# One more merged pair in each half of w_out, with all of w_out's weight sums made earlier and read back from DRAM

## The chip, the cores and the metric

The kernel runs on one core of a Trainium2 chip. The metric is the device time of one execution in microseconds (us), here the median of three runs. The engines named below are PE (TensorE, matmuls; PEld is its loading of the stationary operand), DVE (VectorE), ACT (ScalarE), POOL (GpSimd) and SP, which only issues DMAs. SP works through its DMA issues and its waits in one order; a wait holds up everything that stands behind it.

## The reference

One decoder layer on 256 tokens of width 2048: two attentions side by side, gated and merged, a projection w_out, and a gated MLP.

```python
h = rms_norm(x, attn_norm_g)
proj = h @ w_in
(q_sb, k_sb, v_sb, q_ds, k_ds, v_ds, q_ix, k_ix, w_ix, g_sb, g_ds) = jnp.split(proj, IN_OFFSETS, axis=-1)
...
merged = (jax.nn.sigmoid(g_sb) * (o_sb @ w_branch[:SB_W])
          + jax.nn.sigmoid(g_ds) * (o_ds @ w_branch[SB_W:]))
x = x + merged @ w_out
h = rms_norm(x, ffn_norm_g)
u = causal_depthwise_conv(h @ w_up, conv_w, conv_b)
gate, val = jnp.split(u, 2, axis=-1)
x = x + (jax.nn.silu(gate) * val) @ w_down
```

## The kernel before

**Stages.** In order of time: a short start; five row blocks of w_in (two computed chunk by chunk, three with merged pairs); four column groups of w_in for the first attention's q and k ("heads"); eight column groups for the gates, with one head of each attention worked in between ("gates"); four groups of w_branch; w_out in two halves of 1024 columns; eleven groups of w_up; w_down.

**Products.** Every weight is split into a rounded part hi (by ACT) and a rest lo (by DVE), and every product of a 128 x 128 tile with 512 columns is three matmuls: hi with hi, the left side's rest with hi, hi with the weights' lo. The weights go through a pipeline of *chunks*, numbered through the whole kernel: SP loads a chunk of 512 KB into a raw buffer, ACT writes hi[c % 4], DVE writes lo[c % 4], PE uses both. ACT may write hi of chunk c only when PE has done chunk c - 4 (semaphore w_used), and DVE counts up lo_done. ACT and DVE run three chunks ahead of PE (AHEAD = 3). In the chunked stages SP may refill a raw buffer once lo of the chunk four before is done.

**Plain and merged pairs.** In three row blocks, w_out and w_down, the 16 (w_out) row tiles of the weights are taken in pairs. A *plain* pair is 2 chunks and 8 products (2 row tiles x 2 token halves x 2 column halves). A *merged* pair (kind "summed") does the same 2 x 2 x 2 block product with 7 products in 4 chunks: 1, 2, 2 and 2 products. It needs sums of the weights' four blocks (s13, s24: 4 x 128 x 512) and sums of the left side (left_m for w_out), and its partial results go to four "far" PSUM banks which are copied out and joined by DVE afterwards (far_copy, then out_sums, renamed out_far by the change).

**w_out before.** OUT_SUMMED = 3 merged and 5 plain pairs per half, in the order of OUT_ORDER. Each step's two row tiles are loaded whole (load_step) into six raw buffers: raw0 to raw3 and raw45m. DVE makes the weight sums between its lo's, in weight_sums, from the two raw tiles: one operation of 1024 columns and two of 512. x is loaded again into y by POOL, in quarters, each behind a count of w_used.

**Sums made ahead.** For w_down the sums are made long before they are used. In the gates and the first branch group SP loads the three pieces of a w_down pair into pre_gates (load_terms: 512 + 256 + 256 KB), DVE adds in place (weight_terms: three operations at j = 5, 6, 7 of gates_body), and SP stores 1 MB to the DRAM tensor sums. One such round goes with each group of eight chunks: load at j = 0, store at j = 6 of the next group's loads (gates_turn). The stages of w_up do the same with two buffers. In w_down a merged pair with stored sums loads 256 KB and three times 512 KB.

Of the kernel before, what the change touches and what calls it, by code (L numbers as in the profile page):

```python
# [29 lines left out]
def hybrid_layer(nc, x, positions, attn_norm_g, w_in, q_norm_g, k_norm_g, w_branch, w_out,  # L30
# [51 lines left out]
    OUT_SUMMED = 3  # L82
# [5 lines left out]
    def block_steps(orders, chunk, raw):  # L88

        table = []  # L90
        for b, order in orders.items():
            for kind, pair in order:
                made = pair if kind == "summed" else None
                table.append(Step(b, pair, made, chunk, raw + 2 * len(table)))
                chunk += 2 if made is None else 4
            assert chunk == BLOCK_END[b]
# [7 lines left out]
    OUT_ORDER = [[("plain", 4)] + turns(0, 5, 1, 6, 2, 3) + [("plain", 7)],  # L104
                 turns(0, 4, 1, 5, 2, 6) + [("plain", 3), ("plain", 7)]]
    ROW_STEPS = block_steps({b: ROW_ORDER for b in S_BLOCKS}, ROWS_AT[2], 0)
    ROW_RAWS = 2 * len(ROW_STEPS)
    OUT_STEPS = block_steps({b: OUT_ORDER[b - NB] for b in OUT_BLOCKS}, C_OUT, ROW_RAWS)
    OUT_RAWS = 2 * len(OUT_STEPS)
    PART = {s.chunk + k: (s, k) for s in ROW_STEPS + OUT_STEPS  # L110
            for k in range(2 if s.made is None else 4)}
    ROW_S = [s for s in ROW_STEPS + OUT_STEPS if s.made is not None]
    OUT_FIRST = OUT_STEPS[1]
    FAR_LAST = {b: [s for s in ROW_S if s.m == b][-1].chunk for b in BLOCK_END}
    ROW_LOADS = ROW_RAWS // (SLOTS + 2)
    ROW_SAVED = (C_HEADS - ROWS_AT[2]) // SLOTS - ROW_LOADS
    OUT_EXTRA = (OUT_RAWS - 2 * SLOTS) // (SLOTS + 2)
    OUT_SAVED = (C_UP - C_OUT) // SLOTS - OUT_EXTRA - 2
    ROW_SLOT = [(q + SLOTS) % (SLOTS + 2) for q in range(ROW_RAWS)]
    ROW_SLOT += [q if q < SLOTS else q % SLOTS if q >= OUT_RAWS - SLOTS else q % (SLOTS + 2)  # L120
                 for q in range(OUT_RAWS)]

    def first_turn(q):

        if q < ROW_RAWS:
            return ROWS_AT[2] // SLOTS if ROW_SLOT[q] < SLOTS else 0
        return C_OUT // SLOTS - ROW_SAVED if ROW_SLOT[q] < SLOTS else ROW_LOADS
# [33 lines left out]
    IN_GATES = len(GATE_SUMS)  # L161
    LAST_GROUP = STORED + 1
# [21 lines left out]
    def raw_turn(q):  # L184

        slot = RAW_SLOT[q]
        if slot < SLOTS:
            turn = C_DOWN // SLOTS - ROW_SAVED - OUT_SAVED
        else:
            turn = ROW_LOADS + OUT_EXTRA if slot < SLOTS + 2 else 0  # L190
        return turn + RAW_SLOT[:q + 1].count(slot)
# [32 lines left out]
    with ctx:  # L224
# [9 lines left out]
        def sem(name):  # L234
# [82 lines left out]
        ssum13 = [at("hsum13", [2 * GRP], 74 * KB), at("msum13", [2 * GRP], 64 * KB)]  # L317
        ssum24 = [at("hsum24", [2 * GRP], 78 * KB), at("msum24", [2 * GRP], 68 * KB)]
        raw45m = at("raw45m", [2, 2 * GRP], 72 * KB)
        raw_s = [raw + [at("raw4h", [2 * GRP], 82 * KB), at("raw5h", [2 * GRP], 199 * KB)],  # L320
                 raw + [raw45m[:, 0, :], raw45m[:, 1, :]]]
# [41 lines left out]
        pre_gates = at("pre_gates", [4 * GRP], 48 * KB)  # L363
        sums = nc.dram_tensor("sums", (len(SUM_ROWS) * P, 4 * GRP), f32, kind="Internal").ap()
        leftb = [at(f"leftb{b}", [1, 4, 2, P] if b == SINGLE else [2, 3, 2, P], left_at[b], f32r)
# [199 lines left out]
        def _(sp):  # L565
# [34 lines left out]
            load_tail(3)  # L600
            for b in range(2):
                for g in range(2):
                    load_group(ROWS_AT[b] + g * CPG, w_in, 0,
                               2 * BLOCK + (NB - 1 - b) * BLOCK + g * GRP)
            def load_step(step, w, col):

                for k in range(2):
                    q = step.raw + k
                    slot, old = ROW_SLOT[q], ROW_BEFORE[q]
                    if old is not None:  # L610
                        was = (ROW_STEPS + OUT_STEPS)[old // 2]
                        wait_alone(sp, lo_done, was.chunk + old % 2 + 1)
                        if was.made is not None:
                            wait_alone(sp, (sum13_done, sum4_done)[old % 2],
                                       ROW_S.index(was) + 1)
# [4 lines left out]
                    kt = 2 * step.pair + k  # L620
                    load(slot, raw_s[stage(step)][slot][:, :],
                         w[kt * P:(kt + 1) * P, ds(col, BLOCK)])
# [5 lines left out]
            def load_terms(dst, landed, row, col):  # L628

                sp.dma_start(dst[:, 0:2 * GRP], w_down[ds(row, P), col:col + BLOCK])\  # L630
                    .then_inc(landed, 16)
                sp.dma_start(dst[:, 2 * GRP:3 * GRP], w_down[ds(row + P, P), col + GRP:col + BLOCK])\
                    .then_inc(landed, 16)
                sp.dma_start(dst[:, 3 * GRP:4 * GRP], w_down[ds(row + P, P), col:col + GRP])\
                    .then_inc(landed, 16)

            def gates_turn(i):
# [4 lines left out]
                def before(j):  # L642
                    if j == 0:
                        wait_alone(sp, pre_stored[0], 16 * i + 1)
                        load_terms(pre_gates, pre_landed[0], 2 * P * pair, m * BLOCK)
                    if j == 6:
                        wait_alone(sp, pre_summed, 3 * i + 3)
# [4 lines left out]
            prime(sp, *pre_stored)  # L652
            load_group(C_GATES, w_in, 0, GATE_AT)
            for g in range(1, 8):
                load_group(C_GATES, w_in, CPG * g, GATE_AT + GRP * g, before=gates_turn(g - 1))
            load_group(C_BRANCH, w_branch, 0, 0, before=gates_turn(IN_GATES - 1))
            with sp.Fori(1, 4) as g:
                load_group(C_BRANCH, w_branch, CPG * g, GRP * g)
            for step in OUT_STEPS:
                load_step(step, w_out, (step.m - NB) * BLOCK)  # L660
            def pre_load(m, n):

                wait_alone(sp, pre_stored[m], 16 * n + 1 + (16 * IN_GATES - 16) * (1 - m))
# [6 lines left out]
            def pre_store(m, n):  # L670

                wait_alone(sp, pre_summed, 3 * IN_GATES + 6 * n + 3 * m)
# [31 lines left out]
            wait_alone(sp, pre_stored[0], 16 * LAST_GROUP + 1 + 16 * IN_GATES)  # L704
            up_loads(LAST_GROUP + 1, {(0, 4): lambda: pre_store(1, LAST_GROUP)})
            wait_alone(sp, pre_stored[1], 16 * (LAST_GROUP + 1) + 1)
# [36 lines left out]
        def _(act):  # L743
# [71 lines left out]
            def chunk_hi(c):  # L815
# [5 lines left out]
                if step.made is None or k < 2:  # L821
# [3 lines left out]
                elif k == 2:  # L825
                    src = ssum13[stage(step)]
                    act.wait_ge(sum13_done, ROW_S.index(step) + 1)
                else:
                    src = ssum24[stage(step)]
# [86 lines left out]
            def block_out(c):  # L916

                for b, end in BLOCK_END.items():
# [11 lines left out]
                    if c == last + 7:  # L930
                        act.wait_ge(w_used, last + 4)
                        far_copy(b, 2)
                    if c == end + 2 and b != NB + 1:
# [136 lines left out]
            for c in range(C_OUT + AHEAD, C_UP + AHEAD):  # L1070
# [5 lines left out]
                if 18 <= c - OUT_AT[1] < 22:  # L1076
                    square(c - OUT_AT[1] - 18)
# [159 lines left out]
        def _(dve):  # L1237
# [106 lines left out]
            def chunk_lo(c):  # L1344
# [5 lines left out]
                if step.made is None or k < 2:  # L1350
                    src = raw_s[stage(step)][ROW_SLOT[step.raw + k]]
                else:
                    src = (ssum13, ssum24)[k - 2][stage(step)]
# [6 lines left out]
            def weight_sums(c):  # L1360

                for n, step in enumerate(ROW_S):
                    first_at = step.chunk - (1 if stage(step) else 2)
                    second_at = step.chunk + (1 if stage(step) and step.made == 1
                                              else 0 if stage(step) else -1)
                    b1, b2 = [raw_s[stage(step)][ROW_SLOT[step.raw + k]] for k in range(2)]
                    s13, s24 = ssum13[stage(step)], ssum24[stage(step)]
                    if c == first_at:
# [4 lines left out]
                        dve.wait_ge(left_done, 2 * stage(step) + 2)  # L1373
                        slot = ROW_SLOT[step.raw]
                        if slot < SLOTS or stage(step):
# [1351 lines left out]
```

## Time and profile before

| | us |
|---|---|
| median of 3 runs (lowest to highest) | 1428.06 (1427.55 to 1429.13) |
| the profiled execution's own time | 1428.88 |
| its span in the trace | 1427.0 |

| engine | busy us | share of the span |
|---|---|---|
| PE | 1420.3 | 100% |
| PEld | 1216.2 | 85% |
| DVE | 1192.5 | 84% |
| ACT | 899.4 | 63% |
| POOL | 328.0 | 23% |

DMA moved 350.15 MB, 245 GB/s over the span. A matmul's end is modelled in the trace, so a busy PE hides short waits; the distance from one start to the next says what a matmul costs, and the waits of PE and PEld say who was late. The first matmuls of four stages: w_branch at 535.8 us, w_out at 624.8, w_up at 709.1, w_down at 1201.0; the first sum load of the gates goes out at 335.5.

### The profile page before, as it was taken

What the parts mean: (1) busy time and instruction counts of PE and PEld (TensorE: products, weight loads), DVE (VectorE), ACT (ScalarE), POOL (GpSimd) and SP (SyncE); (2) the same over time, 40 slices, a digit from 0 to 9 for tenths busy, and PEclk for the clock granted to TensorE, in tenths of its full rate; (3) what the DMA queues carried; (4) which work ended last, traced back from release to release, by engine and by line L of the source; (5) the groups of instructions that cost most, each with busy time, mean ns of one, the idle gap of its engine ahead of it and who ended that gap; (6) DMA issues with size and microseconds to landing.
All of it is one profiled execution on the core that took longest, in us unless ns stands there. A gap on an engine that the chain in (4) does not pass through costs nothing.

```text
span 1427.0 us, 23539 instructions
## 1 busy us (share of the span) xinstructions
PE 1420.3 (100%) x7589; PEld 1216.2 (85%) x7589; DVE 1192.5 (84%) x1581; ACT 899.4 (63%) x1298; POOL 328.0 (23%) x365
## 2 busy tenths in 40 slices
PE   9999999999999999999999999999999999999999
PEld 7888888888888888888888888888888888888877
DVE  6778998887767666889978888988889879898998
ACT  6545667566767766666665555555555556675775
POOL 2310000423232223660012222323223322100000
PEclk9999999999999999999999999999999999999999
DMA  8665665666777866567678888888888867798896
GB/s 257 187 195 174 211 197 182 195 185 204 253 249 236 256 229 208 190 208 243 197 237 276 270 297 289 281 278 279 292 289 274 280 221 236 230 321 311 314 331 253
DMA packets 144396, 350.15 MB, mean 245 GB/s; under 512 B 13280, under 2 KB 13568, under 8 KB 140880
## 3 DMA queue, kind: packets, MB, share of 16 engines
q1 hardware_dynamic: 143264, 346.86, 73.9%
q0 software_dynamic: 896, 2.42, 0.6%
q8 instruction: 29, 0.48, 0.1%
q14 instruction: 31, 0.25, 0.0%
q10 hardware_dynamic: 176, 0.14, 0.0%
HBM read 318.96 MB, written 30.41 MB: 245 GB/s over the span
## 4 chain that ended last, share of the span: by engine, by line
PE 97%; DVE 1%; DMA 1%; ACT 0%; POOL 0%; issue 0%; DVEq 0%; POOLq 0%; ACTq 0%; SPq 0%
PE bank L2244 96%; DMA raw<-sums 1%; DVE lo L1906 1%; PE bank L2298 0%; ACT hT L770 0%; PE bank L2522 0%; PE bank L2317 0%; PE bank L2563 0%; DVE whole L1858 0%; ACT hi L1189 0%; DVE y L1932 0%; PE bank L2386 0%; POOL lo L2045 0%; ACT hi L753 0%; DVE leftb L1894 0%
## 5 line engine op out<-in xcount | busy, mean ns | idle before, releaser
L1242 DVE TENSOR_TENSOR lo<-raw,hi 128x1024 fp32r<-128x1024 f32 x338 | 436.8, 1298 | 162.0 <-ACT hi L753 160.4
L753 ACT ACTIVATE hi<-raw 128x1024 fp32r<-128x1024 f32 (+1 forms) x342 | 358.9, 1052 | 262.4 <-PE bank L2244 255.7
L2244 PE MATMUL bank<-h2T,hi 128*128 128x512 f32 x1408 | 483.3, 394 | 0.0
L2244 PE MATMUL bank<-h2T,lo 128*128 128x256 f32 x1408 | 376.8, 278 | 0.0
L2244 PEld LDWEIGHTS bank<-h2T,hi 128*128 128x128 f32 x1408 | 257.9, 188 | 53.5
L2244 PE MATMUL bank<-hT,hi 128*128 128x512 f32 (+1 forms) x784 | 272.9, 395 | 0.8 <-POOL lo L2045 0.7
L2244 PEld LDWEIGHTS bank<-h2T,lo 128*128 128x128 f32 x1408 | 264.5, 188 | 7.8
L2244 PE MATMUL bank<-hT,lo 128*128 128x256 f32 (+1 forms) x784 | 212.6, 281 | 0.0
L1189 ACT ACTIVATE hi<-raw 128x1024 fp32r<-128x1024 f32 (+1 forms) x139 | 132.7, 974 | 65.2 <-PE bank L2244 60.3
L2244 PEld LDWEIGHTS bank<-hT,hi 128*128 128x128 f32 (+1 forms) x784 | 143.9, 187 | 30.6 <-POOL lo L2045 1.3
L1906 DVE TENSOR_TENSOR lo<-raw,hi 128x1024 fp32r<-128x1024 f32 (+1 forms) x139 | 152.3, 1124 | 17.3 <-ACT hi L1189 13.3
L2244 PE MATMUL bank<-hi,hT 128*128 128x512 f32 x520 | 161.7, 392 | 0.0
L2215 POOL TENSOR_TENSOR u<-u,rms_row 128x256 f32<-128x256 f32 x88 | 88.6, 1007 | 278.0 <-DVE u L1777 278.0
L2244 PEld LDWEIGHTS bank<-hT,lo 128*128 128x128 f32 (+1 forms) x784 | 147.0, 187 | 4.0
L2244 PE MATMUL bank<-hi,ffT 128*128 128x512 f32 x486 | 149.8, 389 | 0.0
L2244 PEld LDWEIGHTS bank<-hi,hT 128*128 128x128 f32 x520 | 96.5, 188 | 20.7 <-DVE lo L1356 0.5
L2244 PEld LDWEIGHTS bank<-hi,ffT 128*128 128x128 f32 x486 | 91.1, 188 | 19.3 <-DVE lo L1906 0.4
L2244 PE MATMUL bank<-lo,hT 128*128 128x512 f32 x260 | 101.3, 390 | 0.0
L1787 DVE SCALAR_TENSOR_TENSOR conv<-u,params,conv 128x256 f32<-128x256 f32 x176 | 88.0, 500 | 11.0 <-DVE conv L1787 0.2
L2244 PE MATMUL bank<-lo,ffT 128*128 128x512 f32 x243 | 94.5, 389 | 0.0
L2229 POOL TENSOR_TENSOR conv<-conv,silu 128x256 f32<-128x256 f32 x44 | 60.4, 1372 | 116.3 <-DVE conv L1787 116.3
L2244 PE MATMUL bank<-oT,hi 128*128 128x512 f32 x256 | 86.9, 394 | 0.0
(296 smaller groups left out, 2006.5 us busy)
## 6 DMA issues: line engine op xcount, KB each, us to landing
raw<-in_w_up SPq DMA_DIRECT2D x176, 512.0 KB, 4.6
raw<-in_w_in SPq DMA_DIRECT2D x160, 512.0 KB, 4.2
raw<-in_w_down SPq DMA_DIRECT2D x61, 512.0 KB, 5.9
raw<-sums SPq DMA_DIRECT2D x54, 512.0 KB, 5.8
sums<-pre SPq DMA_DIRECT2D x19, 1024.0 KB, 6.3
raw<-in_w_branch SPq DMA_DIRECT2D x32, 512.0 KB, 3.9
raw<-in_w_out SPq DMA_DIRECT2D x24, 512.0 KB, 5.0
pre<-in_w_down SPq DMA_DIRECT2D x19, 512.0 KB, 4.9
```

The costliest lines, as they stand in the source:

```text
L753: act.activation(hi[s][:, 0:width], raw[s][:, 0:width], ACT.Copy)\
L1189: act.activation(hi[c % SLOTS][:, 0:width], src[:, 0:width], ACT.Copy)\
L1242: dve.tensor_tensor(lo[s][:, 0:width], raw[s][:, 0:width], hi[s][:, 0:width].bitcast(f32), ALU.subtract)\
L1787: dve.scalar_tensor_tensor(conv[b][ct % 2][:, :], u[b][ct][:, k:k + S], params[:, ds(column + e, 1)], conv[b][ct % 2][:, :], ALU.mult, ALU ...
L1906: dve.tensor_tensor(lo[s][:, 0:width], src[:, 0:width], hi[s][:, 0:width].bitcast(f32), ALU.subtract)\
L2215: pool.tensor_tensor(u[b][ct][:, 2:S + 2], u[b][ct][:, 2:S + 2], rms_row[:, :], ALU.mult).then_inc((gate_scaled, val_scaled)[b], 1)
L2229: pool.tensor_tensor(c, c, silu[ct][:, :], ALU.mult).then_inc(act_done, 1)
L2244: return pe.matmul(o, l, r, start=start, stop=stop, skip_group_check=True)
```

## The change

1. **w_out has four merged and four plain pairs per half** (before three and five). Two merged pairs now stand directly behind each other, twice per half: half 0 is p4 s0 s1 p5 s2 s3 p6 p7, half 1 is s0 s1 p4 s2 s3 p5 p6 p7 (s merged, p plain). left_m holds four pairs instead of three.
2. **All eight weight sums of w_out are made earlier**, with load_terms and weight_terms, stored in a new DRAM tensor out_sums and loaded back in w_out (load_step, 256 KB and three times 512 KB for a merged pair). DVE's weight_sums for w_out falls away. Two rounds (IN_ROWS) go through pre_gates in the second row block, six (IN_SPARE) through a new buffer pre_spare in the first six gate groups, beside the w_down sums that are made there already. A gate group's SP order gets one 1 MB store at j = 3 and one 1 MB load at j = 6.
3. **Eight raw buffers in w_out** instead of six (raw67m added); all loads go round robin.
4. **x's quarters**: the counts of w_used behind which POOL loads them stand 5 and 3 chunks apart instead of 3.
5. Some joins move: out_far of half 0 at 7, 16, 17 and 18 chunks behind the last merged pair (before 7, 10, 16, 22), near and square by two chunks with the longer half.

The code, cut to its core:

```diff
-    OUT_SUMMED = 3
+    OUT_SUMMED = 4
...
-    OUT_ORDER = [[("plain", 4)] + turns(0, 5, 1, 6, 2, 3) + [("plain", 7)],
-                 turns(0, 4, 1, 5, 2, 6) + [("plain", 3), ("plain", 7)]]
+    OUT_ORDER = [[("plain", 4), ("summed", 0), ("summed", 1), ("plain", 5), ("summed", 2),
+                  ("summed", 3), ("plain", 6), ("plain", 7)],
+                 [("summed", 0), ("summed", 1), ("plain", 4), ("summed", 2), ("summed", 3),
+                  ("plain", 5), ("plain", 6), ("plain", 7)]]
...
+    OUT_SLOTS = SLOTS + 4
+    IN_ROWS, IN_SPARE = 2, 6
+    OUT_SUMS = [(m, pair) for pair in range(OUT_SUMMED) for m in range(2)]
...
+            def rows_turn(j):
+
+                if j in (0, 10):
+                    wait_alone(sp, pre_stored[0], 1 + 16 * (j // 10))
+                    out_terms(j // 10, pre_gates, pre_landed[0])
+                if j in (8, 15):
+                    e = j // 15
+                    wait_alone(sp, pre_summed, 3 * e + 3)
+                    sp.dma_start(out_sums[e * P:(e + 1) * P, :], pre_gates[:, :])\
+                        .then_inc(pre_stored[0], 16)
...
+            def spare_turn(g, j):
+
+                if j == 3 and 1 <= g <= IN_SPARE:
+                    e = IN_ROWS + g - 1
+                    wait_alone(sp, pre_summed, spare_before(g - 1) + 3)
+                    sp.dma_start(out_sums[e * P:(e + 1) * P, :], pre_spare[:, :])\
+                        .then_inc(pre_stored[1], 16)
+                if j == 6 and g < IN_SPARE:
+                    if g == 0:
+                        wait_alone(sp, w_used, C_HEADS)
+                    wait_alone(sp, pre_stored[1], 16 * g + 1)
+                    out_terms(IN_ROWS + g, pre_spare, pre_landed[1])
...
-                for k in range(2):
+                for k in range(4 if step.stored else 2):
...
+                    elif stage(step) and slot < SLOTS + 2:
+                        wait_alone(sp, sig_done, 8 * 4)
                     elif stage(step):
-                        wait_alone(sp, sig_done, 8 * 4)
+                        wait_alone(sp, left_done, S_BATCHES)
...
+                for e, terms_at in enumerate(((15, 16, 16), (24, 24, 24))):
+                    for k in range(3):
+                        if i == terms_at[k]:
+                            weight_terms(pre_gates, pre_landed[0], 48 * e + 48, 3 * e, k)
...
+                    if spare and j in (3, 4):
+                        for k in ((0,), (1, 2))[j - 3]:
+                            weight_terms(pre_spare, pre_landed[1], 48 * h + 48, 3 * IN_ROWS + 6 * h, k)
...
-                weight_sums(c)
-                for m, joins_at in enumerate(((7, 10, 16, 22), (7, 8, 9, 10))):
+                for m, joins_at in enumerate(((7, 16, 17, 18), (7, 8, 9, 10))):
...
-            for m, used in enumerate((C_OUT + 4, OUT_AT[1] + 2)):
+            for m, used in enumerate((C_OUT + 6, OUT_AT[1] + 6)):
...
-                        pool.wait_ge(w_used, used + 3 * (2 * t + h))
+                        pool.wait_ge(w_used, used + (5 - 2 * m) * (2 * t + h))
```

How it moves instructions, at three places.

SP in the gates, one round from the load of a w_down pair to the next one. Before (raw are the weight chunks, L630 to L634 the three loads of a pair, L648 the store):

```order
L630 DMA pre_gates<-in_w_down 128x1024 [waits pre_stored0]
L632 DMA pre_gates<-in_w_down 128x512
L634 DMA pre_gates<-in_w_down 128x512
L567 DMA raw_59<-in_w_in 128x2x512 [waits lo_done] x2
L567 DMA raw_60<-in_w_in 128x2x512 [waits lo_done] x2
L567 DMA raw_59<-in_w_in 128x2x512 [waits lo_done] x2
L648 DMA sums<-pre_gates 128x2048 [waits pre_summed]
L567 DMA raw_60<-in_w_in 128x2x512 [waits lo_done] x2
L630 DMA pre_gates<-in_w_down 128x1024 [waits pre_stored0]
```

After (L626 to L630 the loads of a pair, L695 the w_down store, L704 the new store):

```order
L626 DMA pre_gates<-in_w_down 128x1024 [waits pre_stored0]
L628 DMA pre_gates<-in_w_down 128x512
L630 DMA pre_gates<-in_w_down 128x512
L590 DMA raw_59<-in_w_in 128x2x512 [waits lo_done] x2
L590 DMA raw_60<-in_w_in 128x2x512 [waits lo_done]
L704 DMA out_sums<-pre_spare 128x2048 [waits pre_summed]
L590 DMA raw_60<-in_w_in 128x2x512 [waits lo_done]
L590 DMA raw_59<-in_w_in 128x2x512 [waits lo_done] x2
L695 DMA sums<-pre_gates 128x2048 [waits pre_summed]
L626 DMA pre_spare<-in_w_out 128x1024 [waits pre_stored1]
L628 DMA pre_spare<-in_w_out 128x512
L630 DMA pre_spare<-in_w_out 128x512
```

The store from pre_spare stands between the fourth and the fifth weight load, and the three loads into pre_spare stand behind the store from pre_gates and ahead of two weight loads.

SP at the start of w_out. Before (raw45m are the fifth and sixth buffer):

```order
L567 DMA raw_59<-in_w_out 128x1024 [waits lo_done] x2
L567 DMA raw_60<-in_w_out 128x1024 [waits lo_done] x2
L567 DMA raw45m<-in_w_out 128x1024 [waits sig_done] x2
L567 DMA raw_59<-in_w_out 128x1024 [waits lo_done] x2
L567 DMA raw_60<-in_w_out 128x1024 [waits lo_done,sum13_done]
L567 DMA raw_60<-in_w_out 128x1024 [waits lo_done,sum4_done]
L567 DMA raw45m<-in_w_out 128x1024 [waits lo_done] x2
L567 DMA raw_59<-in_w_out 128x1024 [waits lo_done,sum13_done]
```

After:

```order
L590 DMA raw_59<-in_w_out 128x1024 [waits pre_stored1,lo_done]
L590 DMA raw_59<-in_w_out 128x1024 [waits lo_done]
L590 DMA raw_60<-in_w_out 128x512 [waits lo_done]
L590 DMA raw_60<-in_w_out 128x1024 [waits lo_done]
L590 DMA raw45m<-out_sums 128x1024 [waits sig_done] x2
L590 DMA raw67m<-in_w_out 128x512 [waits left_done]
L590 DMA raw67m<-in_w_out 128x1024 [waits left_done]
L590 DMA raw_59<-out_sums 128x1024 [waits lo_done] x2
L590 DMA raw_60<-in_w_out 128x1024 [waits lo_done] x2
```

The first merged pair's third and fourth load are its stored sums, in raw45m, which wait for the last gate (sig_done); raw67m follows at once, and no load waits for sum13_done or sum4_done any more.

DVE in w_out, from the second chunk of the first merged pair. Before (L1377, L1390, L1393 make the sums, msum holds them):

```order
L1356 TENSOR_TENSOR lo_68<-raw_60,hi_64 128x1024 [waits hi_done]
L1356 TENSOR_TENSOR lo_65<-msum_134,hi_61 128x1024 [waits hi_done]
L1356 TENSOR_TENSOR lo_66<-msum_136,hi_62 128x1024 [waits hi_done]
L1356 TENSOR_TENSOR lo_67<-raw45m,hi_63 128x1024 [waits hi_done]
L1356 TENSOR_TENSOR lo_68<-raw45m,hi_64 128x1024 [waits hi_done]
L1377 TENSOR_TENSOR msum_134<-raw_59 128x1024 [waits lo_done,left_done,w_landed1,w_landed0]
L1356 TENSOR_TENSOR lo_65<-raw_59,hi_61 128x512 [waits hi_done]
L1356 TENSOR_TENSOR lo_66<-raw_59,hi_62 128x1024 [waits hi_done]
L1390 TENSOR_TENSOR msum_136<-msum_134,raw_59 128x512 [waits lo_done,sum13_done]
L1393 TENSOR_TENSOR msum_136<-msum_136,raw_59 128x512 [waits sum2_done]
L1356 TENSOR_TENSOR lo_67<-msum_134,hi_63 128x1024 [waits hi_done]
```

After:

```order
L1425 TENSOR_TENSOR lo_68<-raw_60,hi_64 128x1024 [waits hi_done]
L1425 TENSOR_TENSOR lo_65<-raw45m,hi_61 128x1024 [waits hi_done]
L1425 TENSOR_TENSOR lo_66<-raw45m,hi_62 128x1024 [waits hi_done]
L1425 TENSOR_TENSOR lo_67<-raw67m,hi_63 128x512 [waits hi_done]
L1425 TENSOR_TENSOR lo_68<-raw67m,hi_64 128x1024 [waits hi_done]
L1425 TENSOR_TENSOR lo_65<-raw_59,hi_61 128x1024 [waits hi_done]
L1425 TENSOR_TENSOR lo_66<-raw_59,hi_62 128x1024 [waits hi_done]
L1425 TENSOR_TENSOR lo_67<-raw_60,hi_63 128x1024 [waits hi_done]
L1425 TENSOR_TENSOR lo_68<-raw_60,hi_64 128x1024 [waits hi_done]
L1758 TENSOR_TENSOR mT<-br_187,mT 128x256 [waits mT_hi]
L1425 TENSOR_TENSOR lo_65<-raw45m,hi_61 128x512 [waits hi_done]
```

The three sum operations of each merged pair are gone, lo is made from the loaded sums, and two merged pairs follow each other.

## Rows read from the trace of the kernel before

**Rows 1.** The page's part 4: the chain that ended last, shares of the span.
```profile
PE 97%; DVE 1%; DMA 1%; ACT 0%; POOL 0%; issue 0%; DVEq 0%; POOLq 0%; ACTq 0%; SPq 0%
```
**Rows 2.** The time line of PE in w_out: start us, length us, engine, line, operation, tiles.
```profile
657.12 0.62 PE L2244 MATMUL bank<-hi,mT 128*128 128x512 f32 x2
...
657.80 0.62 PE L2244 MATMUL bank<-hi,mT 128*128 128x512 f32 x2
```
**Rows 3.** Tile mT's instructions: count, duration ns min/median/max, first and last start us.
```profile
L2244 PE MATMUL bank<-hi,mT x196: 387/389/496, 624.8 to 708.6; 128*128 128x512 f32 x196
```
**Rows 4.** Waits in 624.5 to 709 us: total us, times, longest us.
```profile
ACT hi L834 <- PE bank L2244: 22.2, 19, 2.1
...
PEld bank L2244 <- DVE lo L1356: 0.5, 2, 0.3
```
**Rows 5.** DVE's groups in 624.5 to 709 us: count, busy us, mean ns, idle before.
```profile
L1356 DVE TENSOR_TENSOR lo<-raw,hi 128x1024 fp32r<-128x1024 f32 x18 | 21.7, 1219 | 1.5 <-ACT hi L834 1.5
...
L1356 DVE TENSOR_TENSOR lo<-raw45m,hi 128x1024 fp32r<-128x1024 f32 x6 | 8.2, 1395 | 0.0
...
L1377 DVE TENSOR_TENSOR msum<-raw 128x1024 f32<-128x1024 f32 x3 | 4.2, 1396 | 0.0
```
**Rows 6.** Windows: length; busy us (instructions) of PE, PEld, DVE, ACT, POOL; clock, DMA share, GB/s.
```profile
413.60:439.30 25.70, 25.70 (x153) 22.76 (x152) 18.11 (x26) 17.90 (x28) 7.72 (x9) 1.00 0.77 244
434.00:446.00 12.00, 12.00 (x72) 10.63 (x71) 8.35 (x14) 10.81 (x16) 1.54 (x3) 1.00 0.92 299
1283.00:1308.00 25.00, 25.00 (x112) 20.71 (x111) 23.33 (x28) 16.60 (x18) 0.00 (x0) 1.00 0.97 344
624.50:666.40 41.90, 41.90 (x185) 34.19 (x184) 38.76 (x52) 25.79 (x34) 12.56 (x12) 1.00 0.80 268
666.40:708.80 42.40, 42.40 (x192) 35.17 (x191) 40.68 (x51) 28.27 (x40) 2.15 (x4) 1.00 0.63 196
80.00:125.00 45.00, 45.00 (x236) 36.93 (x235) 32.80 (x48) 23.85 (x33) 3.24 (x6) 1.00 0.56 174
```
**Rows 7.** The time line of SP's DMA issues in the gates, 411 to 447 us.
```profile
412.14 0.40 SPq L630 DMA_DIRECT2D pre_gates<-in_w_down  x1
...
432.11 0.36 SPq L648 DMA_DIRECT2D sums<-pre_gates  x1
...
437.87 0.41 SPq L630 DMA_DIRECT2D pre_gates<-in_w_down  x1
```
**Rows 8.** The DMA view's issues: count, KB each, median us to landing.
```profile
raw<-in_w_in SPq DMA_DIRECT2D x160, 512.0 KB, 4.2
...
sums<-pre_gates SPq DMA_DIRECT2D x8, 1024.0 KB, 4.8
...
pre_gates<-in_w_down SPq DMA_DIRECT2D x8, 512.0 KB, 5.2
...
raw45m<-in_w_out SPq DMA_DIRECT2D x8, 512.0 KB, 4.6
```
**Rows 9.** The time line of ACT in the gates, with idle time before and its releaser.
```profile
445.62 1.06 ACT L753 ACTIVATE hi<-raw 128x1024 fp32r<-128x1024 f32 x1 [0.82 <-PE bank L2244]
448.40 1.06 ACT L753 ACTIVATE hi<-raw 128x1024 fp32r<-128x1024 f32 x1 [1.71 <-PE bank L2244]
```
**Rows 10.** The time line of DVE in the gates.
```profile
449.49 1.23 DVE L1242 TENSOR_TENSOR lo<-raw,hi 128x1024 fp32r<-128x1024 f32 x1 [1.32 <-ACT hi L753]
```
**Rows 11.** Tile pre_gates: DVE's sums, count, duration ns min/median/max, first and last start us.
```profile
L1625 DVE TENSOR_TENSOR pre_gates<-pre_gates x8: 1421/1426/1426, 347.6 to 527.8; 128x1024 f32<-128x1024 f32 x8
L1629 DVE TENSOR_TENSOR pre_gates<-pre_gates x8: 684/684/684, 351.4 to 531.5; 128x512 f32<-128x512 f32 x8
```
**Rows 12.** The time line of SP's DMA issues at the start of w_out.
```profile
623.60 0.80 SPq L567 DMA_DIRECT2D raw45m<-in_w_out  x2
```
**Rows 13.** The time line of ACT at the start of w_out.
```profile
627.76 1.06 ACT L834 ACTIVATE hi<-msum 128x1024 fp32r<-128x1024 f32 x1 [1.45 <-PE bank L2244]
```
**Rows 14.** The time line of DVE in the second row block, with idle time before.
```profile
95.27 1.23 DVE L1242 TENSOR_TENSOR lo<-raw,hi 128x1024 fp32r<-128x1024 f32 x1 [2.65 <-ACT hi L753]
```

More of the change, by code:

```diff
@@ L93, in block_steps @@
                 made = pair if kind == "summed" else None
-                table.append(Step(b, pair, made, chunk, raw + 2 * len(table)))
+                table.append(Step(b, pair, made, chunk, raw, stored and made is not None))
                 chunk += 2 if made is None else 4
+                raw += 4 if table[-1].stored else 2
             assert chunk == BLOCK_END[b]
@@ L161, in hybrid_layer, with spare_before, gates_before @@
     IN_GATES = len(GATE_SUMS)
+    IN_BUFFER = (IN_ROWS + IN_GATES, IN_SPARE)
+    IN_ALL = sum(IN_BUFFER)
+    def spare_before(g):
+        return 3 * IN_ROWS + 6 * g
+    def gates_before(g):
+        return 3 * IN_ROWS + 3 * g + 3 * (IN_SPARE if isinstance(g, int) and g >= IN_SPARE else g + 1)
     LAST_GROUP = STORED + 1
@@ L600, in _, with load_terms, out_terms @@
             load_tail(3)
+            def load_terms(dst, landed, row, col, w=w_down):
+                sp.dma_start(dst[:, 0:2 * GRP], w[ds(row, P), col:col + BLOCK])\
+                    .then_inc(landed, 16)
+                sp.dma_start(dst[:, 2 * GRP:3 * GRP], w[ds(row + P, P), col + GRP:col + BLOCK])\
+                    .then_inc(landed, 16)
+                sp.dma_start(dst[:, 3 * GRP:4 * GRP], w[ds(row + P, P), col:col + GRP])\
+                    .then_inc(landed, 16)
+            def out_terms(e, dst, landed):
+                m, pair = OUT_SUMS[e]
+                load_terms(dst, landed, 2 * P * pair, m * BLOCK, w_out)
+            def rows_turn(j):
[7 more added lines that the diff above has]
+                        .then_inc(pre_stored[0], 16)
+            prime(sp, *pre_stored)
             for b in range(2):
@@ L932, in block_out @@
                         far_copy(b, 2)
+                    if c == end + 2 and b == S_BLOCKS[0]:
+                        act.wait_ge(pre_stored[0], 16 * IN_ROWS + 1)
                     if c == end + 2 and b != NB + 1:
@@ L1362, in weight_sums @@
                 for n, step in enumerate(ROW_S):
[L1363 to L1368, printed above, removed]
+                    b1, b2 = [raw_s[0][ROW_SLOT[step.raw + k]] for k in range(2)]
+                    s13, s24 = hsum13, hsum24
+                    if c == step.chunk - 2:
                         for q in (step.raw, step.raw + 1):
@@ L1662, in gates_body @@
                                           ALU.subtract).then_inc(stay_lo_done, 1)
+                    if spare and j in (3, 4):
+                        for k in ((0,), (1, 2))[j - 3]:
+                            weight_terms(pre_spare, pre_landed[1], 48 * h + 48, 3 * IN_ROWS + 6 * h, k)
                     if j in (5, 6, 7):
-                        weight_terms(pre_gates, pre_landed[0], 48 * h + 48, 3 * h, j - 5)
+                        before = 3 * IN_ROWS + 3 * h + (3 * h + 3 if spare else 3 * IN_SPARE)
+                        weight_terms(pre_gates, pre_landed[0], 48 * (IN_ROWS + h) + 48, before, j - 5)
+                if not spare:
+                    dve.wait_ge(pre_stored[1], 16 * IN_SPARE + 1)
                 column_sums(part_done, col_done, A, part, 16 + 4 * h,
```

165 lines of the change are left out of this document (88 added, 77 removed).

## The prediction

> **What bounds the kernel now.** The chain that ended last is read first: 97% of it is PE [rows 1]. Then PE's time line in w_out: a product is three matmuls, and 657.12 to 657.80 is one, 0.68 us [rows 2]. w_out's matmuls start from 624.8 to 708.6 us [rows 3]; its 122 products (2 x (3 x 7 + 5 x 8)) at 0.68 make 83.0 us, so PE runs nearly without a gap there. The waits say the same from the other side: PE waited for DVE 0.5 us in all of w_out, while ACT waited for PE 22.2 us [rows 4]. So only fewer matmuls shorten the kernel, and anything that makes a weight chunk late by more than its lead lengthens it. DVE is busy 38.76 of 41.90 and 40.68 of 42.40 us in w_out's halves [rows 6]: nearly full, yet not late.
>
> **The change, part by part.**
>
> *One more merged pair per half.* Each saves one product: 2 x 0.68 = **1.36 us less on PE**, all on the path. What PE waited for in w_out (0.5 us) is the most that can come on top.
>
> *DVE's sums leave w_out.* A merged pair's sums cost 1.40 us for the first operation [rows 5] and 0.68 for each of the two half as wide, as where the same is done in pre_gates [rows 11]: 2.76 us, and 6 x 2.76 = 16.6 us. Against that a merged pair makes lo for 3.5 full widths where a plain one makes 2: 2 x 1.5 x 1.22 = 3.7 us more [rows 5]. DVE's 79.4 us in w_out fall to about 66.5 of 83. That buys nothing by itself, as PE waited for only 0.5 us; it pays for the next part.
>
> *Two merged pairs behind each other.* In such a stretch PE needs 7 x 0.68 = 4.8 us for 3.5 widths of lo, DVE 3.5 x 1.22 = 4.3 us and ACT less. DVE keeps up with 0.5 us to spare per pair, and ACT may write hi of a chunk only when PE is done four chunks earlier, so the lead shrinks to a fraction of a microsecond; other DVE work in between (mT, the far joins, 0.68 us each) eats that. I take 0.2 us of PE waits in total, between 0 and 1.2 us (0.3 us, half a far join, at each of four such stretches).
>
> *w_out's loads.* A merged pair loads 1.84 instead of 1.05 MB, 8 x 0.79 = 6.3 MB more. The stage moved 268 x 41.9 + 196 x 42.4 = 19.5 MB [rows 6]; 25.8 MB in 82 us is 315 GB/s, and 344 GB/s were moved over 25 us of w_down while PE stayed full [rows 6]. The tight place is the start: the fifth load waits for the last sigmoid and goes out at 623.60 [rows 12]; it takes 4.6 us [rows 8], lands at 628.2, and is now the third chunk of the first merged pair, whose hi was made at 627.76 [rows 13]. It is late by 0.4 us against ACT; hi and lo then end at 628.2 + 1.06 + 1.22 = 630.5. PE, whose first chunk's end released that hi at 627.5, has seven more products ahead of this chunk and comes to it at 632.3: nothing on PE.
>
> *Two rounds in the second row block.* 4.2 MB more where 174 GB/s at a share of 0.56 are moved [rows 6]: hidden. DVE's three operations (1.43 + 0.68 + 0.68 = 2.8 us [rows 11]) stand for the second round behind the chunk ahead of 95.27 us, where DVE idled 2.65 us [rows 14]. SP's second store waits for them, and behind it the block's last weight load and the first merged pair's loads, each up to 3 us plus the store's own time later; DVE's lead of several chunks there covers it. 0, up to 0.5 us.
>
> *Six rounds in the gates: the term that can decide.* A gate round runs from load to load, 412.14 to 437.87, 25.7 us [rows 7], in which 244 x 25.7 = 6.27 MB are moved at a DMA share of 0.77 [rows 6]. One more load and store of 1.05 MB each make **8.37 MB, 326 GB/s**. What the queue can do is bounded by rows: 299 GB/s at a share of 0.92 (434 to 446 us) is 325 at full share, 244 at 0.77 is 317, 344 at 0.97 in w_down is 355 [rows 6]. A round then takes 8.37/0.325 = 25.8, 26.4 or 23.6 us of service. I take 325, the nearest row, which is the gates' own mixture at its busiest: 0.1 us too much per round, 0.6 us over six rounds. This lateness reaches PE only through the lead. ACT's hi starts when PE has ended the chunk four back (445.62, 448.40: one chunk is 2.78 us [rows 9]); lo follows at 449.49 and ends at 450.72 [rows 10]; PE gets there after three more chunks, 448.2 + 3 x 2.78 = 456.5. So lo is about 6 us ahead, and ACT waits for PE, not for a landing. Within a round the worst place is j = 6: the 1 MB store (4.8 us to land now [rows 8]) is now followed by the 1 MB load, so that the two weight loads behind it land 1.05/0.325 = 3.2 us plus three issues of 0.45 us later, 4.6 us: inside the 6. SP's waits for the new store (j = 3) and for its landing (j = 6) hold weight loads up by the DVE operations in front, under 2.5 us, in the quiet part of the round (the load next takes 4.2 us [rows 8] of some 8). DVE has 18.1 of 25.7 us busy [rows 6] and gets 2.8 more. So: **0 us on PE**; at 317 GB/s 6 x 0.7 = 4.2 us, still inside the lead; at 355 nothing.
>
> The Trainium skill (DMA: Bandwidth & Descriptors, "Where 436 GB/s comes from") puts the limit for transfers between HBM and SBUF at about 358 GB/s per core; by it, as an estimate, the round would need 8.37/0.358 = 23.4 us and have 2.3 us to spare, against 0.1 us too much by the gates' own rows. The sum is 0 by either, but the page's figure would leave the first rival no place; w_down's 355 speaks for it and the gates' 325 against.
>
> *x's quarters and joins*: the last quarter of half 1 goes out at OUT_AT[1] + 15 of 24 chunks and is needed by DVE at chunk 22, some 7 us of PE later; the far copies and squares keep their distance to the end of w_out. 0.
>
> **Sum.** -1.36 + 0.2 = -1.2 us. The profiled execution took 1428.88 us with a span of 1427.0 (1.9 us lie around it) and would become 1427.7; the median of 1428.06 becomes **1426.9 us**, 0.08% less. About 0.2% (2.9 us) is what a measurement of this kernel tells from no change.
>
> **Rivals.**
> 1. *The gates become DMA-bound, slower.* Place: the six rounds with two sums. It decides from where six rounds' excess is more than the lead of 6 us, the 1.2 us gained and the 2.9 us of the bound: 10.1/6 = 1.7 us per round, 8.37/27.4 = 305 GB/s. For it: the gates' rows give 317 to 325 at full share, only 4 to 6% above, and writes to DRAM double there. Against it: shares rise less than the rate when the queue is never empty, as w_down shows. Price at 295 GB/s: 28.4 us a round, 6 x 2.7 = 16 - 6 = 10 us on PE: 1437 us. Chance 0.12.
> 2. *w_out's double merged pairs starve on lo or on loads.* For it: DVE's lo from raw45m took 1.40 us on average where the others took 1.22 [rows 5]. At 1.40 us a pair needs 4.9 us of DVE against 4.8: with the joins about 0.5 us at each of four places, 2 us, so that the gain is used up: 1428.7. That is still no change. Chance 0.15.
> 3. *The change doesn't do what it says*: the saved products are replaced by waits at the same places (far banks not free, sums not landed), so 1428.1. The far copies stand at the same distance from the end, which speaks against it. Chance 0.05, no change.
> 4. *Faster by more than 0.2%*: this needs 1.7 us beyond the matmuls, and PE waited for 0.5 us in w_out. Chance 0.04, about 1425.
> The forecast itself: 0.64.
>
> **Range.** Low end: 1428.06 - 1.36 - 0.5 is 1426.2, less 0.5 us that the runs of before lie below their median: 1425.7. High end: rival 2 with 1428.7, plus 0.5 us of the row blocks and 1.1 us that the runs lie above: 1430.3. Rival 1 lies outside, as does rival 4 in part. Chances: faster 0.04, within 0.2% 0.84, slower 0.12.
>
> **What would show it.** In the profile after: w_out's first to last matmul about 82.7 us; the gate round still 25.7 us, its DMA share near 1 in the first six rounds, and ACT's hi there still released by PE; should hi be released by a DMA landing in rounds 4 to 6, with the round longer than 25.7 us, rival 1 is right. Waits of PEld for DVE's lo of more than 1 us in w_out would be rival 2. The prediction is wrong if the row blocks or the heads change in length, which nothing here touches beyond DMA.

## The result and the profile after

The changed kernel takes **1433.74 us** (median of six runs, 1433.36 to 1434.38) against 1427.74 us for the kernel before beside it: 1.0041 times, 95% interval 1.0028 to 1.0054. The prediction was 1426.9 us with a range up to 1430.3, so it was wrong, on the slower side. The profiled execution has a span of 1431.6 us against 1427.0, 4.6 us more where the medians differ by 6.0: the profiled execution of the kernel before took 1428.88 us, 1.1 us above the median beside the changed kernel.

Lengths of the stages, each from the start of the last matmul of the stage ahead to the start of its own last one, worked out from PE's matmuls in the two traces (us):

| stage | before | after | difference |
|---|---|---|---|
| start | 16.57 | 16.25 | -0.3 |
| row blocks, heads | 312.28 | 312.21 | -0.1 |
| gate round 1 | 25.41 | 26.75 | +1.3 |
| gate rounds 2 to 6, each | 25.73 | 26.92 to 26.94 | +1.2 |
| gate rounds 7 and 8, each | 25.73 | 25.73 | 0 |
| branch | 90.16 | 90.16 | 0 |
| w_out, half 0 and half 1 | 41.86 + 42.43 | 40.82 + 41.73 | -1.7 |
| w_up | 491.95 | 491.95 | 0 |
| w_down | 222.27 | 221.61 | -0.7 |
| end | 3.93 | 4.03 | +0.1 |

All of the loss, **7.3 us**, lies in the six gate rounds that make a spare sum; the two rounds without one have the old length. w_out gained 1.74 us. The 0.3 us of the start and the 0.7 us of w_down are not the change's: kernels below that are the kernel before in both stages have 16.3 and 221.3 us there too.

The waits of the kernel after in the gates (330 to 545 us; who waited for whom: us in all, times, longest) name the place:

```profile
ACT hi L820 <- PE bank L2320: 57.8, 39, 3.7
...
PEld bank L2639 <- POOL prob L2238: 7.2, 6, 1.4
PE bank L2639 <- POOL prob L2238: 6.3, 6, 1.3
```

In each of the six rounds TensorE waits 1.15 to 1.4 us for prob, which POOL (GpSimd) scales by pinv; the two lines, of the weight load and of the matmul, show the same stretch twice and are not to be added. ACT's hi is still released by PE, not by a landing, so the weights are not late. PE's time line in round 3 (start us, length us, engine, line, operation) shows the hole: 399.31 to 400.59, where the kernel before has 422.88 to 423.00 (its round 4; its rounds 2 to 8 are alike).

```profile
399.31 0.27 PE L2320 MATMUL bank<-stay_lo,neg_one_r 128*128 128x128 f32 x1
400.59 0.55 PE L2639 MATMUL bank<-ident,prob 128*128 128x128 f32 x3 [1.01 <-POOL prob L2238]
```

```profile
422.88 0.28 PE L2244 MATMUL bank<-stay_lo,neg_one_r 128*128 128x128 f32 x1
423.00 0.52 PE L2563 MATMUL bank<-ident,prob 128*128 128x128 f32 x3
```

Now POOL and DVE at that place, after:

```profile
396.62 3.92 POOL L2238 TENSOR_SCALAR prob<-prob,pinv 128x128 f32<-128x128 f32 x2 [2.49 <-DVE pinv L1729]
```

```profile
396.25 0.16 DVE L1729 RECIPROCAL pinv<-psum_e 128x2 f32<-128x2 f32 x1
396.33 0.54 DVE L1731 TENSOR_TENSOR stay_lo<-stay,stay_hi 128x384 fp32r<-128x384 f32 x1
396.78 1.22 DVE L1611 TENSOR_TENSOR pre_spare<-pre_spare 128x1024 f32<-128x1024 f32 x1
397.92 1.31 DVE L1311 TENSOR_TENSOR lo<-raw,hi 128x1024 fp32r<-128x1024 f32 x1
399.15 0.68 DVE L1615 TENSOR_TENSOR pre_spare<-pre_spare 128x512 f32<-128x512 f32 x1
399.86 0.77 DVE L1619 TENSOR_TENSOR pre_spare<-pre_spare 128x512 f32<-128x512 f32 x1
```

and before, with DVE's next row behind stay_lo:

```profile
420.19 1.62 POOL L2162 TENSOR_SCALAR prob<-prob,pinv 128x128 f32<-128x128 f32 x2 [2.49 <-DVE pinv L1659]
```

```profile
419.90 0.54 DVE L1661 TENSOR_TENSOR stay_lo<-stay,stay_hi 128x384 fp32r<-128x384 f32 x1
420.98 1.46 DVE L1242 TENSOR_TENSOR lo<-raw,hi 128x1024 fp32r<-128x1024 f32 x1 [0.54 <-ACT hi L753]
```

The same two scalings of POOL (128 and 256 columns) take 3.92 us instead of 1.62. Before, DVE was idle for 0.54 us behind stay_lo, prob was done at 421.81, and PE came for it at 423.00: 1.19 us to spare. After, DVE goes from stay_lo through the sum's first addition, chunk 4's lo and the other two additions to 400.63 with no more than 0.03 us idle, POOL ends at 400.54, and PE, which could have come at 399.43 (0.12 us behind 399.31, as before), goes on at 400.59.

In w_out (the rows that answer to [rows 4] and [rows 6]) PE waits for nothing at all, and DMA is at its share of 1.00 in the first half:

```profile
ACT hi L901 <- PE bank L2320: 18.0, 22, 2.1
...
ACT hi L901 <- DMA raw<-in_w_out: 0.9, 1, 0.9
```

```profile
631.50:672.30 40.80, 40.80 (x182) 33.75 (x181) 31.06 (x41) 27.47 (x36) 10.51 (x12) 1.00 1.00 374
672.30:714.00 41.70, 41.70 (x189) 34.62 (x188) 38.34 (x47) 29.95 (x42) 2.15 (x4) 1.00 0.79 259
```

### The profile page after: what moved, and what is told of

It is laid out like the page before. It is cut to its first block, busy times and chain, and to the rows that moved or that the text cites. A ratio compares the mean times of both kernels' runs of the same rounds, so it can differ in the third digit from the quotient of the medians.

```text
span 1431.6 us, 23622 instructions
## 1 busy us (share of the span) xinstructions
PE 1419.1 (99%) x7583; PEld 1215.9 (85%) x7583; DVE 1204.8 (84%) x1591; ACT 902.8 (63%) x1302; POOL 340.4 (24%) x365
## 4 chain that ended last, share of the span: by engine, by line
PE 94%; ACT 2%; issue 1%; POOL 1%; DVE 0%; DVEq 0%; POOLq 0%; ACTq 0%
PE bank L2320 93%; ACT hi L820 1%; POOL prob L2238 1%; ACT L1068 1%; PE bank L2374 0%; ACT prob L1068 0%; PE bank L2639 0%; PE bank L2598 0%; ACT hT L837 0%; PE bank L2393 0%; DVE lo L1311 0%; DVE y L2008 0%; PE bank L2462 0%; POOL lo L2121 0%; ACT L820 0%
```

## The experiments

Three theories fit this reading. **A**: the additions keep DVE busy in one unbroken row just where POOL scales prob, POOL does not get on beside them, and PE waits for POOL. **B**: it is the doubled traffic of the gate rounds. **C**: it is DVE's 2.8 us more of work in a round, which make something of DVE's own late.

### The additions one chunk later

```diff
-                    if spare and j in (3, 4):
-                        for k in ((0,), (1, 2))[j - 3]:
+                    if spare and j == 4:
+                        for k in range(3):
                             weight_terms(pre_spare, pre_landed[1], 48 * h + 48, 3 * IN_ROWS + 6 * h, k)
```

> The changed kernel, with all three additions of a spare sum put behind chunk 4's lo of a gate round instead of one behind chunk 3's and two behind chunk 4's. The transfers are the same bytes in the same places. Theory A (GpSimd's scaling of prob is kept waiting by VectorE's unbroken row of additions, and TensorE waits for prob): the scaling gets done under chunk 4's lo as in the kernel before, the six long gate rounds go from 26.93 us back to about 25.73, TensorE's waits for prob (13.5 us by the wait view from 330 to 545 us) go, and the time is 1433.7 - 7.3 = about 1426.4 us. Rival B (the traffic of the sums in the rounds is what lengthens them): rounds 26.9, 1433.7 us. Rival C (VectorE is late with lo because it has 2.8 us more to do in a round): the same work in the round, so 26.9 and 1433.7 us.

Measured: 1427.38 us, 0.9999 times before (0.9990 to 1.0008). Rounds 2 to 6 are 25.73 us, with every byte still moved; round 1 is 26.44. The window of one round has the answer to rival 1 (columns as in [rows 6]): 327 GB/s at a DMA share of 0.90, PE busy throughout.

```profile
380.73:406.46 25.73, 25.73 (x154) 22.79 (x152) 21.27 (x29) 17.93 (x28) 7.85 (x9) 1.00 0.90 327
```

The same work of DVE and the same traffic, at another place, cost nothing in five of the six rounds: B and C fall for these. The expected 1426.4 was missed by the first round: there chunk 4's lo starts 0.30 us behind stay_lo, before the first scaling is done (0.54 us and just after it in the other rounds), the additions follow that, and PE waits for prob once.

```profile
PEld bank L2639 <- POOL prob L2238: 1.1, 1, 1.1
PE bank L2639 <- POOL prob L2238: 0.9, 1, 0.9
```

### The traffic without the additions, and the additions without the traffic

```diff
-                            weight_terms(pre_spare, pre_landed[1], 48 * h + 48, 3 * IN_ROWS + 6 * h, k)
+                            weight_terms(pre_spare, pre_landed[1], 48 * h + 48, 3 * IN_ROWS + 6 * h, k, 8)
...
+                    dve.tensor_tensor(p[:, 0:cut], p[:, 0:cut], p[:, GRP:GRP + cut],
+                                      ALU.add).then_inc(pre_summed, 1)
```

> The changed kernel, with each of the three additions of the spare sums cut to 8 columns, in the same places with the same waits; the loads and stores of the spare sums stay whole. It leaves the spare sums out (what it stores for six of w_out's eight merged pairs are no sums). Theory A and rival C: VectorE has 0.3 us instead of 2.8 there, the rounds go back to about 25.73 us and the time to about 1426.4. Rival B (traffic): rounds stay 26.9, 1433.7 us.

Measured: 1425.85 us, 0.9986 (0.9977 to 0.9995); all rounds 25.73, the first 25.39; no wait of PE in the gates.

```diff
+            def idle_add(n, width):
...
+                dve.tensor_tensor(idle_[:, 0:width], idle_[:, 0:width], idle_[:, 0:width],
+                                  ALU.add).then_inc(bias_raw, 1)
...
+                    if j in (3, 4):
+                        for i, width in enumerate(((1024,), (512, 512))[j - 3]):
+                            idle_add(3 * h + 1 * (j - 3) + i + 1, width)
                     if j in (5, 6, 7):
```

> The kernel before, with three additions of VectorE on memory that nothing else uses, 1024 columns behind chunk 3's lo and twice 512 behind chunk 4's, in all eight gate rounds; no transfer is added. Theory A and C: all eight rounds become 26.9 us, 8 x 1.2 = 9.6 us more: 1437.4 us; A says with PE waiting for prob from GpSimd, C with PE waiting for lo. Rival B: no bytes, no change: 1427.7 us.

Measured: 1438.48 us, 1.0076 (1.0060 to 1.0091). The kernel before becomes 10.7 us slower by additions whose result nobody reads, with 26.92 to 26.94 us per round behind the first, and the waits are those of the changed kernel, now in eight rounds:

```profile
PEld bank L2575 <- POOL prob L2174: 9.5, 8, 1.4
PE bank L2575 <- POOL prob L2174: 8.3, 8, 1.2
```

B is out. C, if it means that lo is late, is out as well: PE waits for prob, not for lo. Besides the 9.7 us in the rounds, this trace has 1.3 us more in the branch (91.45 us instead of 90.16), without a wait; matmuls follow each other there at a pitch about 1.4% longer. The kernel below with the first addition alone has it too; the other kernels, the changed one among them, have not, and where it comes from stays open.

### Prob scaled by ScalarE

```diff
-                    pool.tensor_scalar(prob[:, k0:k1], prob[:, k0:k1], pinv[:, t:t + 1], None,
-                                       ALU.mult).then_inc(prob_done, 1)
...
+                    if j == 4:
+                        act.wait_ge(pinv_done, h + 1)
+                        for t, (k0, k1) in enumerate(((0, P), (P, KEYS))):
+                            act.activation(prob[:, k0:k1], prob[:, k0:k1], ACT.Copy,
+                                           scale=pinv[:, t:t + 1]).then_inc(prob_done, 1)
```

> The changed kernel, with the scaling of prob by pinv made by ScalarE (two activations behind chunk 4's hi, estimated at 0.4 and 0.5 us from the Exp of the same shapes) instead of GpSimd; VectorE's additions and all transfers stay as they are. Theory A: prob is ready about 1.5 us behind pinv whatever VectorE does, the six rounds go back to about 25.73 us, and the time is about 1426.4 us. Rivals B and C: the traffic and VectorE's row are the same, rounds 26.9, 1433.7 us or somewhat more for ScalarE's 0.9 us a round.

Measured: 1425.99 us, 0.9989 (0.9979 to 0.9998). The rounds are 25.73, the first 25.31, with DVE's row and the traffic of the changed kernel untouched. ScalarE needs 0.79 us for both scalings:

```profile
394.63 0.79 ACT L1079 ACTIVATE prob<-prob,pinv 128x128 f32<-128x128 f32 x2
```

The control makes the same edit in the kernel before.

> The kernel before with the scaling of prob made by ScalarE instead of GpSimd, the same edit as in e6_prob_on_act. TensorE did not wait for prob before, so theory A expects no change: 1427.7 us, and what e6_prob_on_act gains on the kernel before (1.75 us) is then w_out's. If the move to ScalarE itself shortens something, about 1426.

Measured: 1427.49 us, 0.9997 (0.9987 to 1.0007): nothing. So the gain of the version above is the change's own, from w_out, set free by taking prob away from POOL.

### How much of the row is needed

The first addition alone at j = 3 (the tuple for chunk 4 emptied), and all three at j = 4, both in the kernel before:

> The kernel before, with only the 1024-wide addition on unused memory behind chunk 3's lo in all eight gate rounds (the two 512-wide ones behind chunk 4's lo left out). Theory A: VectorE's unbroken row behind pinv is then stay_lo, the addition and chunk 4's lo, and ends some 1.4 us before the row of e3_idle_3_and_4; the second scaling ends at the row's end and 0.4 us, which is about when TensorE comes: PE loses 0 to 0.4 us a round, so 1427.7 to 1430.9 us, against 1438.5 with all three. Should the addition at this place alone be enough (GpSimd slowed by whatever stands right behind pinv), the rounds are 26.9 as there and the time 1437 to 1438 us.

Measured: 1434.29 us, 1.0048 (1.0031 to 1.0064); rounds of 26.41 (the first 26.22), that is 0.68 us more each, and the 1.3 us in the branch. The expectation of 0 to 0.4 us was too low. In that trace the row ends with lo at 398.29 and the second scaling at 399.08, 0.79 us later (DVE's lo, then POOL); I had taken the 0.4 us by which the first, half as wide, ended behind the operation it waited for. So the loss is between the two ends that were set: the row's length counts, not the mere presence of an addition behind pinv.

```profile
396.98 1.31 DVE L1243 TENSOR_TENSOR lo<-raw,hi 128x1024 fp32r<-128x1024 f32 x1
```

```profile
395.68 3.40 POOL L2174 TENSOR_SCALAR prob<-prob,pinv 128x128 f32<-128x128 f32 x2 [2.49 <-DVE pinv L1668]
```

> The kernel before, with all three additions on unused memory (1024, 512, 512 columns) behind chunk 4's lo in all eight gate rounds. Theory A: between stay_lo and chunk 4's lo VectorE is idle for 0.5 us and the second scaling gets in there, so rounds of 25.73 us; only the first round, where chunk 4's lo follows stay_lo at once, waits about 1 us as in e1_sums_at_4: 1428.7 us. If it is the amount of VectorE's work in a round that counts, 8 x 1.2 us more as in e3_idle_3_and_4: 1438 us.

Measured: 1428.62 us, 1.0005 (0.9995 to 1.0015); rounds 2 to 8 are 25.73 and the first 26.44, as expected. The same amount of DVE work costs 10.7 us at one place (9.7 of them in the rounds) and 0.9 at the other.

### The same row from reductions

Against the kernel with three additions on unused memory:

```diff
-                dve.tensor_tensor(idle_[:, 0:width], idle_[:, 0:width], idle_[:, 0:width],
-                                  ALU.add).then_inc(bias_raw, 1)
+                dve.tensor_reduce(idle_[:, 1023:1024], idle_[:, 0:width], AX.X, ALU.max)\
+                    .then_inc(bias_raw, 1)
...
-                        for i, width in enumerate(((1024,), (512, 512))[j - 3]):
+                        for i, width in enumerate(((1020,), (512, 512))[j - 3]):
```

> e3_idle_3_and_4 with the three additions on unused memory made reductions of the same widths (maximum over 1020, 512 and 512 columns into one column), which read one operand instead of two and write next to nothing, and should keep VectorE busy for about as long (by the two reductions over 128 columns of a round, 0.3 us each with what an instruction costs, estimated at 1.1 and 0.6 us). Theory A1 (an operation of VectorE that reads two operands from SBUF keeps GpSimd from reading): the scaling gets in beside the reductions, PE loses 0 to 0.3 us a round, 1427.7 to 1430 us. Theory A2 (any work of VectorE slows GpSimd, or VectorE's being busy delays something else that TensorE waits for): rounds 26.9, 1438 us as in e3_idle_3_and_4.

Measured: 1427.45 us, 0.9999 (0.9989 to 1.0009), rounds of 25.73 (the first 25.31) and no wait of PE for prob. Its time lines of DVE and POOL:

```profile
419.57 0.54 DVE L1670 TENSOR_TENSOR stay_lo<-stay,stay_hi 128x384 fp32r<-128x384 f32 x1
420.03 1.21 DVE L1640 TENSOR_REDUCE idle__218<-idle__218 128x1 f32<-128x1020 f32 x1
421.15 1.22 DVE L1243 TENSOR_TENSOR lo<-raw,hi 128x1024 fp32r<-128x1024 f32 x1
422.28 1.41 DVE L1640 TENSOR_REDUCE idle__218<-idle__218 128x1 f32<-128x512 f32 x2
```

```profile
419.86 1.62 POOL L2174 TENSOR_SCALAR prob<-prob,pinv 128x128 f32<-128x128 f32 x2 [2.49 <-DVE pinv L1668]
```

DVE's row is nearly as long and as unbroken as with the additions (1.21 us against 1.22 for the first, 1.41 against 1.48 for the other two), and POOL needs its old 1.62 us. So it is not DVE being busy that stops POOL: an operation with two operands from SBUF does, one with a single operand does not.

A reduction also writes one column where an addition writes as many as it reads, and the experiment does not part the two. The trace of the last experiment below does. There POOL's copy ds_v runs once beside additions of DVE with one operand in PSUM (bank) and one in SBUF (part), which write 256 columns each, and once, in round 7, beside an operation with both operands in SBUF. DVE, then POOL:

```profile
410.92 1.41 DVE L1641 TENSOR_TENSOR gates<-bank,part 128x256 f32 x4
...
520.59 1.30 DVE L1647 TENSOR_TENSOR gates<-gates,rms_row 128x1024 f32 x1
```

```profile
411.70 0.40 POOL L2230 COPY ds_v<-tok 128x256 f32 x1
...
520.76 1.39 POOL L2230 COPY ds_v<-tok 128x256 f32<-128x256 f32 x1
```

The copy keeps its 0.40 us beside the former and takes 1.39 beside the latter. So in these rows it is the second operand from SBUF and not the writing that holds POOL up.

### The additions two chunks later

```diff
-                    if spare and j in (3, 4):
-                        for k in ((0,), (1, 2))[j - 3]:
+                    if spare and j == 5:
+                        for k in range(3):
                             weight_terms(pre_spare, pre_landed[1], 48 * h + 48, 3 * IN_ROWS + 6 * h, k)
```

> The changed kernel, with all three additions of a spare sum behind chunk 5's lo of a gate round, ahead of pre_gates' first addition. Theory A: the scaling of prob is done by then in every round, the first one too (in e1_sums_at_4 it waited 1.0 us there, since chunk 4's lo came right behind stay_lo and the additions right behind that); GpSimd's next work, the mask on stick, is then the one beside the additions, and TensorE reads stick only 6 us after it was ready in e1_sums_at_4 (400.1 and 406.5 us), so nothing new waits: 25.3 us for the first round and 25.73 for the others, 1427.4 - 1.0 = 1426.4 us. The other way: VectorE's row of 4 us at that place makes chunk 6's lo late or stick late, and a round is longer than 25.73 us.

Measured: 1436.16 us, 1.0054 (1.0040 to 1.0067). Wrong by ten microseconds, and worse than the changed kernel: rounds 2 to 6 are 27.2 to 27.7 us, and round 7, which makes no sum, is 26.35. Waits in the gates, of PE and ACT, then of SP's queue:

```profile
ACT hi L820 <- DMA raw<-in_w_in: 22.9, 11, 2.9
...
PEld bank L2639 <- POOL prob L2238: 6.8, 5, 1.5
PE bank L2639 <- POOL prob L2238: 6.1, 5, 1.3
...
PEld bank L2320 <- DVE gates L1641: 2.1, 5, 0.4
```

```profile
SPq L571 <- DVE pre_spare L1619: 47.4, 6, 8.0
```

SP's store of the sum waits for the third addition, and weight loads stand behind it in SP's queue. With the additions at j = 4 SP waited 30.8 us for them in all; at j = 5 it waits 47.4, up to 8.0 at a time. In round 3 the store goes out at 406.49 us and three weight loads behind it at 406.93 to 408.76; with j = 4, where round 3 begins 1.0 us earlier, the store goes out at 400.71 and the loads at 401.15 to 404.53. Hi then waits for landings (22.9 us in all, 3.7 with j = 4), lo and pinv come late, chunk 4's lo follows stay_lo without the hole, and prob is again kept waiting (scaling from 398.27 to 400.94). It looks as the prediction's first rival would, hi released by a landing, but the rate is not the cause: the version with j = 4 moves the same bytes at 327 GB/s with 3.7 us of such waits and none of them passed on to PE. That SP's order is the cause is read from the trace and was not tried apart.

## Why the prediction was wrong

**The step that failed is "Six rounds in the gates".** It found the right place ("the term that can decide") and asked whether the weights get late: by the DMA rate, by SP's waits, by lo's lead of 6 us. The answer to that held: PE waited for no lo there, although SP's wait for the new store was 3.9 us a round and not under 2.5. The sentence "DVE has 18.1 of 25.7 us busy [rows 6] and gets 2.8 more", with its "0 us on PE", is the hole. It priced DVE's additions by DVE's idle time and asked who waits for DVE. It did not ask who works beside DVE at j = 3 and 4. POOL is not named anywhere in the working, because it is off the chain and idle most of the time; but PE needs its prob once a round, with 1.19 us to spare. That row, prob's scaling from 420.19 to 421.81 and PE's transposes at 423.00, stood in the trace of before. In place of 0 the term measured 1.3 + 5 x 1.2 = 7.3 us.

That DVE and POOL slow each other could have been read there too: the lo beside the second scaling took 1.46 us, where lo otherwise took 1.22 [rows 5]. The first round of the kernel before shows it best: there chunk 4's lo starts 0.31 us behind stay_lo instead of 0.54, the two scalings take 2.56 us instead of 1.62, 0.79 us beyond that lo's end as in the kernel with the first addition alone, and of the 1.19 us to spare 0.05 are left (345.71 to 345.76).

```profile
343.15 2.56 POOL L2162 TENSOR_SCALAR prob<-prob,pinv 128x128 f32<-128x128 f32 x2 [2.50 <-DVE pinv L1659]
```

```profile
345.76 0.55 PE L2563 MATMUL bank<-ident,prob 128*128 128x128 f32 x3
```

The Trainium skill (SBUF — State Buffer, "Who interferes with whom") states it as a rule: a DVE instruction with two inputs in SBUF contends with a GpSimd instruction that reads SBUF, since its second input comes through the read port that both share, while tensor_reduce does not contend. The reductions and the additions above agree with it, 1.62 against 3.92 us. By that rule of the Trainium skill the loser is held until the running instruction ends. Here it was held longer: in the row of 396.33 to 400.63 us the second scaling, free to start from 398.4, ended 1.31 us behind lo, which ended at 399.23, and 0.71 us behind the addition after that. Why it did not get in between the two was not tried and stays open.

The other steps, one by one:

- *One more merged pair per half*, -1.36 us: right. w_out became 1.74 us shorter; the 0.38 us beyond the products fit the 0.5 us that PE waited for lo before [rows 4] and no longer does.
- *DVE's sums leave w_out*: about right in size (66.5 us estimated; 31.06 + 38.34 = 69.4 measured). That it "buys nothing by itself" was wrong by at most those 0.38 us.
- *Two merged pairs behind each other*, 0.2 us: nothing. PE waited for no lo. Rival 2 falls.
- *w_out's loads*, 0: right. ACT waited 1.2 us for two landings, PE for none. 374 GB/s over 40.8 us were moved, more than the 355 that the prediction took from w_down as the most at full share, and more than the 358 that it quotes from the Trainium skill as the limit per core; this kernel runs on one core alone.
- *Two rounds in the second row block*, 0: right, 52.32 us before and after.
- *Rival 1*, the gates DMA-bound: did not happen. Its bound of 325 GB/s at full share was too low: 327 at a share of 0.90 with the additions at j = 4. The chance of 0.12 for slower was for this mechanism alone, so the outcome was given a chance for a reason that was not its own.
- *x's quarters and joins*, 0: no wait of PE in w_out, so right.

The sum with the failed term as measured is -1.74 + 7.3 = +5.6 us; the medians differ by 6.0, and the span shows +4.6, the start and w_down being 1.0 us shorter in this execution.

The views the prediction named for the check (hi's releaser, DMA share, waits for lo) would have told that the round was wrong and not why: the round grew while hi was still released by PE, a case that it did not list.

The version that keeps the change and moves prob's scaling to ScalarE takes 1425.99 us, 1.75 us less than before: close to the -1.2 us of the prediction's sum, which thus was the worth of the change with that one collision removed. At 0.1% the gain is smaller than the 0.2% by which the prediction told faster from no change, though its interval lies below 1.

## What to carry to other kernels

An engine's idle time is not free room: before putting work into it, list what every other engine runs at that place and who waits for the end of that, with its slack in microseconds; an engine that is busy for a quarter of the span can be the one. Two-operand work of VectorE from SBUF belongs away from GpSimd work that TensorE waits for, or one of the two goes to ScalarE. And work whose result a queue waits for has a latest place as well as an earliest one: two chunks later was worse than the collision.

## What was not expected of the hardware

- GpSimd's two scalings of 128x128 and 128x256 take 1.62 us beside VectorE's single-operand reductions and 3.92 us beside two-operand additions of the same length. VectorE pays less: in that row lo takes 1.31 instead of 1.23 us and the third addition 0.77 instead of 0.68, and chunk 5's lo behind the row takes 1.64.
- 374 GB/s were moved over 40.8 us of w_out at a DMA share of 1.00 with TensorE busy throughout.
- GpSimd's other operations swing in the same way without any harm: sb_q's copy took 0.39 us before and in most rounds 1.39 us after.
